# One root for the norms of eight heads instead of two roots for four heads each

## The reference, cut to what matters

```
def l2norm(x):
    return x * lax.rsqrt(jnp.sum(x * x, axis=-1, keepdims=True) + 1e-6)

qkv = jax.nn.silu(causal_dwconv(qkv, conv_w))
q, k, v = jnp.split(qkv.astype(f32), 3, axis=-1)
q = l2norm(q.reshape(shp))
k = l2norm(k.reshape(shp))
...
q = chunks(q) * (Dk ** -0.5)
o = chunk_gated_delta_rule(q, k, v, g, beta)
```

## Time and profile before

| | |
|---|---|
| median of three runs | 3031.56 us |
| the profiled execution, its own time | 3028.52 us |
| its span in the trace | 3026.7 us |
| TensorE busy | 97% |
| VectorE busy | 64% |
| ScalarE busy | 48% |
| mean granted TensorE clock | 0.982 |

### The profile page before, as it was taken

One profiled execution on the slowest core, in us unless ns is written; L12 is line 12 of the kernel. 1 busy time (PEld: TensorE's weight loads), 2 busy tenths in 40 slices (PEclk: granted clock), 3 DMA queues, 4 the chain that ended last, 5 costly groups with the idle time before them and its releaser, 6 DMA issues.

```text
span 3026.7 us, 55781 instructions
## 1 busy us (share of the span) xinstructions
PE 2936.0 (97%) x23624; PEld 2870.5 (95%) x23624; DVE 1939.2 (64%) x2218; ACT 1446.9 (48%) x1817; POOL 195.8 (6%) x166
## 2 busy tenths in 40 slices
PE   8998999999999999999999999999899999999998
PEld 7987989999999999999998999898899999999997
DVE  6467767455667666666777676666655655655665
ACT  5356644444454444444445545544544444444464
POOL 0010011000000000000001021122000000000000
PEclk9999999999999999999999999998999999999999
DMA  6644523665555665666555633221466656666654
GB/s 209 185 120 132 162 70 98 185 184 175 187 181 183 182 184 179 185 187 183 178 181 160 181 112 89 80 84 56 122 182 185 184 179 186 185 183 183 183 171 139
DMA packets 252105, 482.24 MB, mean 159 GB/s; under 512 B 16944, under 2 KB 22320, under 8 KB 251728
## 3 DMA queue, kind: packets, MB, share of 16 engines
q1 hardware_dynamic: 251856, 478.68, 53.1%
HBM read 476.53 MB, written 2.10 MB: 158 GB/s over the span
## 4 chain that ended last, share of the span: by engine, by line
PE 81%; DVE 8%; ACT 5%; DMA 3%; issue 2%; POOL 0%; DVEq 0%; SPq 0%; ACTq 0%
PE psm L411 74%; PE psb L470 8%; DVE slo L325 3%; ACT shi L315 2%; ACT ar L495 2%; DVE ar L498 2%; DMA raw<-in_w_in 1%; DVE ar L506 1%; DVE x L498 1%; PE psb L478 0%; DMA raw<-in_w_out 0%; DMA raw<-in_w_down 0%; ACT gh L495 0%; ACT gf L495 0%; POOL ar L498 0%
## 5 line engine op out<-in xcount | busy, mean ns | idle before, releaser
L325 DVE TENSOR_TENSOR slo<-raw,shi 128x1024 fp32r<-128x1024 f32 (+1 forms) x901 | 1124.5, 1253 | 696.6 <-ACT shi L315 693.9
L315 ACT ACTIVATE shi<-raw 128x1024 fp32r<-128x1024 f32 (+1 forms) x901 | 946.8, 1054 | 1145.0 <-PE psm L411 918.2
L411 PE MATMUL psm<-gh,shi 128*128 128x256 f32 x3664 | 1052.5, 287 | 17.3 <-DVE slo L325 15.0
L411 PE MATMUL psm<-gl,shi 128*128 128x256 f32 x3664 | 1040.8, 284 | 0.0
L411 PE MATMUL psm<-gh,slo 128*128 128x256 f32 x3664 | 1040.5, 284 | 0.0
L411 PE MATMUL psm<-hh,shi 128*128 128x256 f32 x3408 | 977.0, 287 | 13.8 <-DVE hl L515 7.0
L411 PE MATMUL psm<-hh,slo 128*128 128x256 f32 x3408 | 969.5, 284 | 0.0
L411 PE MATMUL psm<-hl,shi 128*128 128x256 f32 x3408 | 969.4, 284 | 0.0
L411 PEld LDWEIGHTS psm<-gh,shi 128*128 128x128 f32 x3664 | 705.8, 193 | 25.3 <-DVE slo L325 16.4
L411 PEld LDWEIGHTS psm<-gl,shi 128*128 128x128 f32 x3664 | 705.8, 193 | 1.0 <-issue 0.3
L411 PEld LDWEIGHTS psm<-gh,slo 128*128 128x128 f32 x3664 | 705.4, 193 | 0.3
(11 more groups left out here) (188 smaller groups left out, 1307.3 us busy)
## 6 DMA issues: line engine op xcount, KB each, us to landing
raw<-in_w_in SPq DMA_DIRECT2D x240, 512.0 KB, 3.7
raw<-in_w_up SPq DMA_DIRECT2D x176, 512.0 KB, 4.1
raw<-in_w_ffn_up SPq DMA_DIRECT2D x128, 512.0 KB, 3.8
raw<-in_w_ffn_down SPq DMA_DIRECT2D x128, 512.0 KB, 4.1
raw<-in_w_down SPq DMA_DIRECT2D x88, 512.0 KB, 4.6
raw<-in_w_out SPq DMA_DIRECT2D x64, 512.0 KB, 4.2
raw<-in_w_ple_gate SPq DMA_DIRECT2D x32, 512.0 KB, 4.5
raw<-in_w_branch_b SPq DMA_DIRECT2D x16, 512.0 KB, 3.9
```

Of the source, the lines that this page charges most:

```text
L315: hi_tok[j] = A.do(lambda e: e.activation(shi[:, s, 0:m], raw[:, q, 0:m], ACT.Copy), landed, pe_tok.get(j - NS), chain=False, cost=0.22 + ...
L325: lo_tok[j] = V.do(lambda e: e.tensor_tensor(slo[:, s, 0:m], raw[:, q, 0:m], shi[:, s, 0:m].bitcast(F), ALU.subtract), landed, hi_tok[j], ...
L411: e.matmul(out, l, r, start=st, stop=sp, skip_group_check=True),
```

## The change

`heads_norm` now stands for one half (`half` 0 is q, 1 is k) and is put in lane 2 once for two groups, at g = 0 and g = 2. It squares and sums the first four heads as before, but copies the sums out of PSUM into the first 256 columns of `rr`; it waits (asking again and again, at the head of lane 2) until the second group's `g_tok` is there, does the same for it into the next 256 columns, and then takes one root over 512 columns. After that come, for each of the two groups in turn, the reciprocal, the four matmuls with `hsel` and the four products.

```diff
-        def heads_norm(g):
-            buf = (gq, gk)[g // 2][:, 4 * (g % 2):4 * (g % 2) + 4, :]
-            sq, rr = hh_f[:, 0:1024].rearrange("p (a b) -> p a b", a=4), hh_f[:, 1024:1280]
-            yield (g_tok[g],)
-            ta = act(sq, buf, ACT.Square, g_tok[g])
+        def heads_norm(half):
+            sq = hh_f[:, 0:1024].rearrange("p (a b) -> p a b", a=4)
+            rr = hh_f[:, 1024:1536].rearrange("p (a b) -> p a b", a=2)
+            b = None
+            for i in range(2):
+                g = 2 * half + i
+                buf = (gq, gk)[half][:, 4 * i:4 * i + 4, :]
+                while g not in g_tok:
+                    yield
+                yield (g_tok[g],)
+                ta = act(sq, buf, ACT.Square, g_tok[g])
+                yield (ta,)
+                b = bank()
+                tp = mms([(b.ap[32 * f:32 * f + 32, 0:256], C("osel"), sq[:, f, :], True, True) for f in range(4)],
+                         ta, *b.free)
+                ta = act(rr[:, i, :], b.ap[:, 0:256], ACT.Copy, tp)
+                b.free = (ta,)
+                yield ()
+            ta = act(rr, rr, ACT.Sqrt, bias=C("eps", 0, 1))
             yield (ta,)
-            b = bank()
-            tp = mms([... C("osel"), sq[:, f, :] ...], ta, *b.free)
-            ta = act(rr, b.ap[:, 0:256], ACT.Sqrt, tp, bias=C("eps", 0, 1))
-            b.free = (ta,)
-            yield (ta,)
-            tv = rec(rr, ta)
-            ...
-            A.wait(tn)
-            qn_tok[g] = tn
+            for i in range(2):
+                g = 2 * half + i
+                buf = (gq, gk)[half][:, 4 * i:4 * i + 4, :]
+                tv = rec(rr[:, i, :], ta)
+                yield (tv,)
+                for f in range(4):
+                    row = slice(32 * f, 32 * f + 32)
+                    b = bank()
+                    tp = mms([(b.ap[:, 0:256], C("hsel")[row, :], rr[row, i, :], True, True)], tv, *b.free)
+                    tn = stt(buf[:, f, :], buf[:, f, :], 128 ** -0.5 if g < 2 else 1.0, b.ap[:, 0:256],
+                             ALU.mult, ALU.mult, tp)
+                    b.free = (tn,)
+                    if f % 2:
+                        yield ()
+                A.wait(tn)
+                qn_tok[g] = tn
...
-                if g < 4:
-                    bgs[2].append(heads_norm(g))
+                if g in (0, 2):
+                    bgs[2].append(heads_norm(g // 2))
```

More of the change, by code:

```diff
@@ L927, in build @@
         g_tok, qn_tok = {}, {}
-        def heads_norm(g):
-            buf = (gq, gk)[g // 2][:, 4 * (g % 2):4 * (g % 2) + 4, :]
-            sq, rr = hh_f[:, 0:1024].rearrange("p (a b) -> p a b", a=4), hh_f[:, 1024:1280]
-            yield (g_tok[g],)
-            ta = act(sq, buf, ACT.Square, g_tok[g])
-            yield (ta,)
-            b = bank()
-            tp = mms([(b.ap[32 * f:32 * f + 32, 0:256], C("osel"), sq[:, f, :], True, True) for f in range(4)],
-                     ta, *b.free)
-            ta = act(rr, b.ap[:, 0:256], ACT.Sqrt, tp, bias=C("eps", 0, 1))
-            b.free = (ta,)
-            yield (ta,)
-            tv = rec(rr, ta)
[L943 to L952, removed]
-            A.wait(tn)
-            qn_tok[g] = tn
+        def heads_norm(half):
[17 more added lines that the diff above has]
+            ta = act(rr, rr, ACT.Sqrt, bias=C("eps", 0, 1))
+            yield (ta,)
+            for i in range(2):
[14 more added lines that the diff above has]
+                qn_tok[g] = tn
```

## The result

The changed kernel takes 3019.86 us (median of five runs, 3017.92 to 3022.38) against 3031.56 (five runs, 3030.52 to 3034.59): ratio 0.996, 95% interval 0.9945 to 0.9974.

A forecast was written before the change was run, and what follows sets the result against it. TensorE was taken as the bound, so side work counts only where it stands. Terms -3.8 + 0.6 + 1.0 - 1.5 + 0.7 = -3.0 us took 3031.56 to about 3028.5 us, range 3020.5 to 3037.

The forecast's parts named there:

- What bounds the kernel, and the mechanism of the two waits: TensorE bounds the span; its waits near 260 and 285 us are for `psb` banks held until VectorE's products read them.
- First place: 243 to 265 us: two loads and the burst at 255 with its waits go; -3.8 us, ends -5.7 and 0.
- The cap by VectorE's 3.75 us: 243 to 265 us: TensorE advances only as far as `slo` does, and VectorE gets rid of 1.75 + 2.00 = 3.75 us.
- Second place: 265 to 290 us: wider ScalarE work +0.6 us, two bursts behind the joint root +1.0, ends -5 and +5.3.
- 6 to 10: Sign for 277 to 285 us: the wait there remains, 6 to 10 us in all, ended by a product of the norm.
- Rival (a): 265 to 290 us: attention is through before the joint burst, term becomes -5; -9.0 in all, 3022.5 us; chance 0.25.
- First k norm: 304 to 330 us: root and 3.75 us of VectorE gone, TensorE's 1.51 us wait near 327 goes; -1.5 us.
- Second k norm: 330 to 350 us: 3.75 us of VectorE and 0.6 of ScalarE come back; +0.7 us, ends 0 and +3.8.
- What comes behind: Start of the recurrence, which waits for v's convolution, two groups of weights after k's norms: no change.
- a move behind 400 us: Sign the prediction is wrong: the time moves in a stage after 400 us, which nothing in it explains.
- a stray layout: Rest of the program laid out anew by the planner; with the slower rival it makes up slower's 0.14.
- From the profiled execution to the median: Whole kernel: the median of the runs is taken as 3.04 us above the profiled execution, giving 3031.56 - 3.0.

The follow-up runs named there:

- before_pairs: Kernel before, each norm's next pair of matmuls and banks taken only after the first pair of products is through: 3019.4 us, ratio 0.9967.
- loads_back: Changed kernel in its own order, root taken at each copy out of PSUM so the four table loads return: 1.1 us behind the changed kernel from q2 to gate3.
- loads_out: Kernel before in its own order, without the root of q's and k's first group, so four table loads less: 3032.0 us, ratio 1.000.
- before_late: Kernel before without ScalarE's wait for the norm's last product at each group's end, the next norm's squares waiting instead: ratio 0.9968.
- loads_out_planned: Kernel before without the first q and k groups' root, the planner told of no load and laying out anew: 3022.48 us, ratio 0.9969.
- a_clock: Changed kernel, no instruction changed, planner's clocks of ScalarE and VectorE put back 3.46 us behind v's second group: 3023.92 us, ratio 0.9978.
- after_late: Changed kernel without ScalarE's wait for the norm's last product at each group's end: loss between v's two groups' scalings falls from 4.66 to 1.96 us.
- b_clock: Kernel before, no instruction changed, planner's clocks behind v's second group put on 3.46 us (ScalarE, VectorE, loads), GpSimd's back 1.83: ratio 0.9974.
- b_clock_m1: Kernel before, no instruction changed, planner's clocks of ScalarE, VectorE and loads put back 1.00 us behind v's second group: ratio 0.9982.

## Why the prediction was wrong, step by step

- **What bounds the kernel, and the mechanism of the two waits: right in the main.** The matmuls waited for banks, with a burst holding three or all four. `before_pairs` shows it for the first wait. Two readings in it were wrong. The 3.44 us at 259.80 ended not by a norm's product but by ScalarE's copy of an attention step, at 259.47, which gave back the fourth bank. And the two table loads do not stand in VectorE's idle 4.96 us: that runs from 274.97 to 279.93, and the second load is over at 274.99. In that time ScalarE does the exponentials and a copy of an attention head and four of the convolution's multiplications, and then the `shi` copy.
- **First place, -3.8: measured -3.84** (q2 to k1). Of it 0.75 by the loads (`loads_back`, and 0.76 by `loads_out`); the rest stays in the changed order with all loads back, and I put it down to the burst that is no longer there. The cap by VectorE's 3.75 us fits, but was not tested.
- **Second place, +0.6 and +1.0: measured -5.00** (k1 to k2). This is the step that failed most, 6.6 us. I took the wait of 7.65 for something that ScalarE's queue there caused and would cause again. It was a clash of one burst with one attention step in one order. The changed kernel's attention is 4 us further, and the waits there are 0.79, 0.31 and 3.32, 4.4 us in all where I had named 6 to 10. Rival (a) named the size (-5) but not this. Its condition, that attention is through before the joint burst, did not hold: an attention matmul still waits 3.32 us at 289.35 behind a product. And three edits without the change, `before_pairs`, `before_late` and `loads_out_planned`, remove or shrink the wait as well.
- **First k norm, -1.5: measured -0.10** from k2 to v1, and -0.97 in `a_clock`, which has the same work and order there. The wait of 1.51 did shrink, to 0.46. But v1's scaling stood in both kernels right behind `slo` on VectorE, not behind TensorE, so this mark doesn't show it; what it brought is within the next term.
- **Second k norm, +0.7: measured +4.66** (v1 to v2), beyond the end of +3.8. I counted what is moved and not who stands behind it: `A.wait(tn)`, which I had read in the first k norm, puts ScalarE's `shi` copies behind a product that VectorE reaches 9 us later. `after_late`, without that wait and in another order, gives 2.7 us of it back.
- **What comes behind: "nothing", measured -4.6** (v2 to gate3, from 351 to 568 us). The prediction counted a move behind 400 us as a sign that it is wrong, and so it is. I had named a stray layout only as a rest in the chances. Three kernels with nothing but clocks changed show 3.4 and 5.5 us won and 5.2 lost by it. What changed here is the lateness of ScalarE and VectorE at one point in the planner's books.
- **From the profiled execution to the median:** I added 3.04 us as if it held for both kernels; the changed one had 0.0.

The terms missed by 6.6 and 4.6 us one way and by 1.4 and 4.0 the other, so that -3.0 became -8.9 by gate3. That the time lies only 0.6 us outside the range is partly luck: three of the five terms were off by more than the whole forecast and in part offset each other.

The four table loads, all the work that the change takes out, are worth 0.8 us in one stretch in a fixed order and none that can be told in the whole. Joining the roots moved a burst away from the attention, and that, with the new order behind it, is the gain. Not fully settled is in which waits the recurrence's layouts differ. From v2 to gate3 TensorE stands 11.8 us before, 10.1 in the changed kernel, 9.8 in `b_clock`, 9.1 in `b_clock_m1` and 13.8 in `a_clock`, where one matmul waits 5.64 us at 479.06 for a VectorE product. The changed kernel's longest wait near that place is 2.36, at 464.10. So `a_clock`'s idle time accounts for 3.7 of its 5.2 us against the changed kernel; for the gains against before it accounts for half or less in two of three cases.

## What to carry to other kernels

Where one program of queues is laid out by estimates, compare two versions with the order held fixed (the real function changed, the planned one kept) before crediting an edit with the difference; and move a planner's clocks by a microsecond, with no edit at all, to see how large a difference means nothing. A background burst that takes every PSUM bank makes all others wait in order on TensorE: in this kernel taking banks by twos, and yielding the result that frees them, ended that. And an engine's wait on something it doesn't read yet is worth trying at its first reader.

## What the runs showed that I had not expected

The same instructions in another order differ by up to 9.5 us, 0.3% of the kernel (`loads_out` 3032.0, `loads_out_planned` 3022.5; their ratios to before, taken on one chip, 1.000 and 0.9969). The stretch in the second block from 1660 to 2188 us, 1300 us behind the change, differed by 2.2 us between two executions in the same order (changed kernel and `loads_back`), and by up to 5.3 us among all; a difference of that size read from one profile of a late stretch means nothing here.
